# One-core encoder block: activations of 16 FFN blocks turned on VectorE and moved by SBUF transfers

## The reference

```python
hn = _modulate(_rms(h, norm_ffn1[l]), sh1, sc1)
h = h + 0.5 * g1[:, None, :] * _swiglu(hn, ffn1_w1[l], ffn1_w3[l], ffn1_w2[l])
...
hn = _modulate(_rms(h, norm_ffn2[l]), sh3, sc3)
h = h + 0.5 * g3[:, None, :] * _swiglu(hn, ffn2_w1[l], ffn2_w3[l], ffn2_w2[l])
```

## Time and profile before

| | |
|---|---|
| time, median of 3 runs | 2528.01 us (2526.07 to 2530.0) |
| span of the profiled execution | 2528.3 us |
| TensorE busy | 2499.9 us, 99% of the span |
| VectorE busy | 1830.6 us, 72% |
| ScalarE busy | 1159.0 us, 46% |
| read from HBM | 608.43 MB, 242 GB/s over the span |
| transposes of `act_tok` on TensorE | 176 |
| granted TensorE clock, mean | 0.998 of full speed |

### The profile page before, as it was taken

How to read it: one execution, slowest core, us unless ns; L and a number is a source line. 1 busy time by engine, 2 the same in 40 slices (tenths; PEclk the granted TensorE clock), 3 DMA queues, 4 the chain that set the end, 5 groups by cost and what they waited for, 6 DMA issues and landing times.

```text
span 2528.3 us, 33298 instructions
## 1 busy us (share of the span) xinstructions
PE 2499.9 (99%) x12314; PEld 2108.9 (83%) x12314; DVE 1830.6 (72%) x2016; ACT 1159.0 (46%) x1396; POOL 84.0 (3%) x118
## 2 busy tenths in 40 slices
PE   7999999999999999999999999999999999999999
PEld 5778888888888999898888888888888888888887
DVE  6876668898877888887866677776689555555556
ACT  4444444444445555655555444444544444444443
POOL 4210000000000000000100000000000000000000
PEclk9999999999999999999999999999999999999999
DMA  9976579898976777874544778787598655565565
GB/s 370 366 282 194 184 261 344 291 341 291 340 259 210 270 261 268 279 228 152 164 142 138 245 267 272 251 298 243 167 334 301 203 192 190 189 191 188 190 191 173
DMA packets 281219, 614.45 MB, mean 243 GB/s; under 512 B 23586, under 2 KB 24196, under 8 KB 280196
## 3 DMA queue, kind: packets, MB, share of 16 engines
q1 hardware_dynamic: 269600, 571.41, 67.4%
q0 software_dynamic: 9744, 36.73, 3.9%
q10 hardware_dynamic: 1748, 4.62, 0.5%
HBM read 608.43 MB, written 4.25 MB: 242 GB/s over the span
## 4 chain that ended last, share of the span: by engine, by line
PE 95%; DVE 2%; DMA 1%; issue 0%; ACT 0%; ACTq 0%; DVEq 0%
PE psum L2159 27%; PE psum L2161 27%; PE psum L2160 27%; PE psum L2453 3%; PE psum L2455 3%; PE psum L2454 3%; PE psum L2476 2%; PE psum L2147 2%; DMA raw<-in_ffn_w 1%; DVE w_lo L1368 1%; PE psum L2269 0%; DVE ada_acc L1482 0%; DMA badas<-in_b_ada 0%; PE psum L2240 0%; PE psum L2201 0%
## 5 line engine op out<-in xcount | busy, mean ns | idle before, releaser
L1368 DVE TENSOR_TENSOR w_lo<-raw,w_hi 128x1024 fp32r<-128x1024 f32 x850 | 1036.6, 1223 | 518.8 <-ACT w_hi L880 517.6
L880 ACT ACTIVATE w_hi<-raw 128x1024 fp32r<-128x1024 f32 x850 | 899.0, 1060 | 1017.4 <-PE psum L2161 873.5
L2159 PE MATMUL psum<-w_hi,xT_hi 128*128 128x512 f32 x1984 | 784.8, 396 | 6.4 <-issue 4.6
L2161 PE MATMUL psum<-w_hi,xT_lo 128*128 128x512 f32 x1984 | 773.8, 390 | 0.0
L2160 PE MATMUL psum<-w_lo,xT_hi 128*128 128x512 f32 x1984 | 773.5, 390 | 0.0
L2159 PEld LDWEIGHTS psum<-w_hi,xT_hi 128*128 128x128 f32 x1984 | 373.1, 188 | 89.8 <-issue 13.1
L2161 PEld LDWEIGHTS psum<-w_hi,xT_lo 128*128 128x128 f32 x1984 | 372.9, 188 | 78.9
L2160 PEld LDWEIGHTS psum<-w_lo,xT_hi 128*128 128x128 f32 x1984 | 373.2, 188 | 75.8
L2159 PE MATMUL psum<-w_hi,aT_hi 128*128 128x512 f32 x704 | 274.8, 390 | 0.0
L2161 PE MATMUL psum<-w_hi,aT_lo 128*128 128x512 f32 x704 | 274.1, 389 | 0.0
L2160 PE MATMUL psum<-w_lo,aT_hi 128*128 128x512 f32 x704 | 274.0, 389 | 0.0
(11 more groups left out here) (260 smaller groups left out, 1904.6 us busy)
## 6 DMA issues: line engine op xcount, KB each, us to landing
raw<-in_ffn_w SPq DMA_DIRECT2D x528, 512.0 KB, 4.5
ada_raw<-in_w_ada SPq DMA_DIRECT2D x224, 512.0 KB, 5.7
raw<-in_w_in SPq DMA_DIRECT2D x224, 512.0 KB, 3.8
ada_raw<-in_w_ada POOLq DMA_DIRECT2D x32, 512.0 KB, 7.4
ada_more<-in_w_ada POOLq DMA_DIRECT2D x32, 512.0 KB, 7.3
raw<-in_w_br_ssd SPq DMA_DIRECT2D x32, 512.0 KB, 5.3
raw<-in_w_br_att SPq DMA_DIRECT2D x32, 512.0 KB, 4.5
raw<-in_w_out SPq DMA_DIRECT2D x32, 512.0 KB, 5.1
```

Source lines behind the costliest of these rows:

```text
L880: nc.scalar.activation(w_hi[:, n.slot(SPLIT), 0:size], raw[:, n.slot(RAW), 0:size], ACT.Copy).then_inc(hi_ready, 1)
L1368: nc.vector.tensor_tensor(w_lo[:, n.slot(SPLIT), 0:size], raw[:, n.slot(RAW), 0:size], w_hi[:, n.slot(SPLIT), 0:size], ALU.subtract).then_ ...
L2159: nc.tensor.matmul(o, hi[:, kt + k, toks], whi, start=a, stop=False)
L2161: ins = nc.tensor.matmul(o, lo[:, kt + k, toks], whi, start=False, stop=b)
```

## The change

In 16 of the 22 blocks (4 to 9 of the first FFN, 0 to 9 of the second) the eight transposes leave TensorE. In their place:

1. VectorE, right behind the product at u = 2, turns `act_tok` in 32x32 pieces (`turn_bands`): two block transposes of 128x512, one for each half of the tokens, into `act_blk`. Each piece is then turned within itself, but lies on the partitions of its token group.
2. SP, behind the load of unit 6 (`MOVE_AFTER`) and the adaLN load that may follow, waits for `act_blocked` and issues 16 transfers of 32 partitions by 256 values (32 KB) from `act_blk` to `aT_raw`, one for each pair of partition groups (`move_act`).
3. ScalarE at u = 7 waits for all 16 (`act_moved`) and writes `aT_hi` from `aT_raw` in two instructions, one for each half (`moved_hi`); VectorE writes `aT_lo` in two (`moved_lo`).
4. On TensorE the wait for `y_added` that stood before the turn stands before the first w2 unit.

Blocks 0 to 3 of the first FFN and block 10 of both keep the turn on TensorE. `turns(o)` counts the turns that are left.

```diff
+BLOCKED_FROM = (4, 0)
+BLOCKED = tuple(FBLK - 1 - o for o in BLOCKED_FROM)
+BANDS = P // 32
+BAND_DMAS = BANDS * BANDS
...
+    act_blk = place("act_blk", at_temp + 64 * KB, [BANDS, UNIT // BANDS])
+    aT_raw = place("aT_raw", at_temp + 68 * KB, [BANDS, UNIT // BANDS])
...
+    MOVE_AFTER = 6
...
+    def blocked(o):
+
+        f, i = divmod(o.n0, FBLK)
+        return BLOCKED_FROM[f] <= i < FBLK - 1
...
+    def by_tokens(t, half):
+
+        return t[:, :, half * P:(half + 1) * P].rearrange("p k (b t) -> p k b t", t=32)
+
+    def by_bands(half):
+
+        return aT_raw[:].rearrange("p b (k s t) -> p s k b t", s=HALF, t=32)[:, half]
...
+        def move_act(o):
+
+            sp.wait_ge(act_blocked, moves_before(o).count(plus=1))
+            for band in range(BANDS):
+                for to in range(BANDS):
+                    sp.dma_start(aT_raw[32 * to:32 * (to + 1), band, :],
+                                 act_blk[32 * band:32 * (band + 1), to, :]).then_inc(act_moved, 16)
...
                 for u, source in enumerate(pair_of_blocks):
...
+                    o = At(f * FBLK + LOOP_FROM[f] + u // BLOCK, 2, trip)
+                    if blocked(o) and u % BLOCK == MOVE_AFTER:
+                        move_act(o)
...
+        def moved_hi(o, n):
+
+            act.wait_ge(act_moved, moves_before(o).count(plus=1) * 16 * BAND_DMAS)
+            act.wait_ge(unit_done, n.count())
+            for half in range(HALF):
+                ins = nc.scalar.activation(by_tokens(aT_hi, half), by_bands(half), ACT.Copy)
+            ins.then_inc(ahi_ready, 1)
...
                     if u == 7:
-                        act_hi(o)
+                        moved_hi(o, n) if blocked(o) else act_hi(o)
...
+        def turn_bands(o):
+
+            dve.wait_ge(prod_ready, o.count(plus=1))
+            for half in range(HALF):
+                ins = nc.vector.transpose(act_blk[:].rearrange("p c (k s t) -> p s k c t", s=HALF, t=32)[:, half],
+                                          act_tok[:, half, :].rearrange("p (k c t) -> p k c t", c=BANDS, t=32))
+            ins.then_inc(act_blocked, 1)
+
+        def moved_lo(o):
+
+            dve.wait_ge(ahi_ready, o.count(plus=1))
+            for half in range(HALF):
+                ins = nc.vector.tensor_tensor(by_tokens(aT_lo, half), by_bands(half), by_tokens(aT_hi, half), ALU.subtract)
+            ins.then_inc(alo_ready, 1)
...
                     if u == 2 and not after_second:
                         prod(o, n)
+                    if u == 2 and blocked(o):
+                        turn_bands(o)
                     if u == 7:
-                        act_lo(o)
+                        moved_lo(o) if blocked(o) else act_lo(o)
...
                 for u in range(UPB):
-                    if u == 5:
+                    if u == 5 and not blocked(o):
 
                         if adds.n0:
                             pe.wait_ge(y_added, adds.count())
...
                     if q == 0:
                         pe.wait_ge(alo_ready, o.count(plus=1))
+                        if blocked(o) and adds.n0:
+                            pe.wait_ge(y_added, adds.count())
```

More of the change, by code:

```diff
@@ L301, in build @@
     act_turned = sem("act_turned")
+    act_blocked = sem("act_blocked")
+    act_moved = sem("act_moved")
     ahi_ready = sem("ahi_ready")
@@ L515, in rows_cols, with moves_before, turns @@
         return w[row:row + 2 * P, cols].rearrange("(k p) n -> p k n", p=P)
+    def blocked(o):
+        f, i = divmod(o.n0, FBLK)
+        return BLOCKED_FROM[f] <= i < FBLK - 1
+    def moves_before(o):
+        f = o.n0 // FBLK
+        return o + (-BLOCKED_FROM[0] if f == 0 else BLOCKED[0] - FBLK - BLOCKED_FROM[1])
+    def turns(o):
+        before = sum(1 for i in range(o.n0) if not blocked(At(i)))
+        return At(before) if blocked(o) else o + (before - o.n0)
     def span(start, size):
@@ L683, in _ @@
                     load_ada(At(e * KT + k), ada_source(e, k))
+                for i, at in enumerate((FIRST, FIRST + SECOND)):
+                    if f and u == at + MOVE_AFTER:
+                        move_act(At(f * FBLK + i))
             with sp.Fori(0, TRIPS[f]) as trip:
@@ L698, in _ @@
                     load_ada(At(e * KT + k % KT), ada_source(e, k % KT))
+                o = At(f * FBLK + FBLK - 3 + u // BLOCK)
+                if blocked(o) and u % BLOCK == MOVE_AFTER:
+                    move_act(o)
             if f == 1:
@@ L1026, in second @@
                     if u == 7:
-                        act_hi(o, 0)
+                        moved_hi(o, n)
             def hidden(n, o):
@@ L1053, in ffn @@
                 if u == 7:
-                    act_hi(At(o))
+                    moved_hi(At(o), At(n)) if blocked(At(o)) else act_hi(At(o))
                 if u == UPB - 1 + LAG:
@@ L1585, in prod @@
             dve.wait_ge(silu_ready, o.count(plus=1))
-            if o.n0:
-                dve.wait_ge(act_turned, o.count())
+            if o.n0 and not blocked(o + -1):
+                dve.wait_ge(act_turned, turns(o).count())
             nc.vector.tensor_tensor(act_tok[:], silu_a[:], psum[:, bank:bank + HALF, :], ALU.mult).then_inc(prod_ready, 1)
+        def turn_bands(o):
[9 more added lines that the diff above has]
+            ins.then_inc(alo_ready, 1)
         def act_lo(o, bank=4, hi=aT_hi, lo=aT_lo):
@@ L1720, in ffn @@
                     prod(At(o), At(n))
+                    if blocked(At(o)):
+                        turn_bands(At(o))
                 if u == 7:
-                    act_lo(At(o))
+                    moved_lo(At(o)) if blocked(At(o)) else act_lo(At(o))
             n += 2 * UPB
@@ L2413, in ffn @@
             for u in range(UPB):
-                if u == 5:
+                if u == 5 and not blocked(At(o)):
                     pe.wait_ge(y_added, adds)
@@ L2425, in ffn @@
                     pe.wait_ge(alo_ready, o + 1)
+                    if blocked(At(o)):
+                        pe.wait_ge(y_added, adds)
                 if i == 1:
```

7 lines of the change are left out of this document (3 added, 4 removed).

## The result

The changed kernel takes 2562.89 us (median of 4 runs, 2561.27 to 2566.81) against 2528.69 for the kernel before: ratio 1.0139, 95% interval 1.0125 to 1.0153. It is slower by 34 us. The forecast was 2517.

A forecast was written before the change was run, and what follows sets the result against it. The prediction took TensorE to bound the kernel (95% of the chain): 2528.3 - 13.9 for removed transposes + 3.2 for stalls in adaLN blocks = 2517.6 us span, say 2517; range 2511 to 2534.

The forecast's parts named there:

- What is removed: On TensorE, 16 blocks lose their eight transposes, 0.87 us a block by the chain: 13.9 us gained.
- What is added on VectorE and ScalarE: Block transposes 1.5 us and low part in halves 0.1 per block on VectorE; some 0.1 on ScalarE, hidden in gaps.
- rival of dear transposes: On VectorE, scattered 32x32 pieces cost say 5 us a block instead of 1.5: 2548 us; chance 0.06.
- What is added on SP: Sixteen 32 KB transfers per block on SP's queue at 0.45 us an issue: 7.2 us per block.
- the broadcast row: The largest issue measured on SP, 1.07 us, used as upper bound per issue; the range took it only to 0.65.
- The hold: Time SP's queue is taken by the 16 issues in a block, delaying loads behind them: 7.2 us.
- A block with adaLN loads: Eight blocks, six in the first FFN, two in the second: 0.4 us lost in each, 3.2 us in all.
- the cover: Time to spare before late loads stop TensorE: 0.7 and 0.1 us with adaLN loads, 2.4 without.
- A block without adaLN loads: Eight blocks of the second FFN: 2.4 us to spare at unit n+7, so the delay is hidden and nothing lost.
- The sum: Whole kernel: 2528.3 - 13.9 + 3.2 = 2517.6 us for the profiled span, say 2517 for the median.
- SP's hold decides: Rival on SP's queue: 2530 us at 0.60 us an issue, 2569 at 0.75; chance 0.19 for 0.6 or more.
- The DMA engines decide: Rival: backlog drains slower than 1.4 us a load, 1.6 us lost in eight blocks, 2527 us; chance 0.10.

The follow-up runs named there:

- no_moves: The changed kernel without the 16 transfers per block, high and low parts made from act_blk; 2515.21 us, ratio 0.9941.
- hbm_source: The changed kernel with all 16 transfers per block fetched from w_ada in HBM, readers taking act_blk; 2533.28 us, ratio 1.0014.
- spread_4x4: The changed kernel with the 16 transfers issued four behind each of the loads of units n+6 to n+9; 2551.21 us, ratio 1.0086.
- pool_moves: The changed kernel with the same 16 transfers issued by GpSimd instead of SP; 2526.37 us, ratio 0.999.
- twelve_moves: The changed kernel with only the first 12 of the 16 transfers per block, readers taking act_blk; 2533.09 us, ratio 1.0016.
- eight_moves: The changed kernel with only the first 8 of the 16 transfers per block, readers taking act_blk; 2521.71 us, ratio 0.9965.
- bounce: The changed kernel with moves through HBM: four stores behind the load of n+6, one fetch behind that of n+8; 2521.88 us, ratio 0.9973.

## Why the prediction was wrong

**What is removed: right.** 13.9 us forecast; no_moves stands 14.7 below the profiled execution before (2528.3 - 2513.6). The chain's 0.87 us for eight transposes was the right reading; eight times 272 ns would have been 2.5 times too much.

**What is added on VectorE and ScalarE: right where nothing is late.** Two block transposes of 0.69 us, hidden in no_moves. The rival of dear transposes fell. But that VectorE has gaps was read for the first FFN alone, and in the first two blocks of the second it has hardly any: before, it was busy 71.0 of the 75 us from 1870 to 1945, in no_moves 73.3.

**What is added on SP: the price of an issue failed.** I took 0.45 us between the rows of back-to-back issue, and measured is 0.633. The rows were good for what they showed, transfers with an end in HBM (0.46 in a row of 16). The one thing that set the moves apart, both ends in SBUF, I did not count among the unknowns: I compared by shape and size, and the bound from the broadcast row, 1.07, I cut down to 0.65 for the range. The hold became 10.3 us instead of 7.2.

**A block with adaLN loads: the cover failed too.** With the hold as forecast, hbm_source loses 18.4 us (2532.0 - 2513.6), not 3.2. In the first FFN the blocks lose 0.5 to 1.7 us instead of 0.4. The backlog drains more slowly at first than the 1.4 us a load that I took from the best slice of the earlier trace rows (4.1 us from n+7 to n+8), and I followed it only to n+9: in three of the six blocks n+8 and n+9 are in time, and TensorE first stands at n+12 for `y_add`, a wait that the prediction put at nothing after its move. In the first two blocks of the second FFN they lose 4.6 and 5.8, more than half of the whole: I had worked out one block of the first FFN and counted these two like it. Yet the trace of before showed that they had less cover; from 1860 to 1960 us ScalarE waited there for weight loads 8 times, 13.4 us in sum, without any move, and in the blocks of the first FFN never:

```profile
ACT w_hi L880 <- PE psum L2161: 41.4, 26, 1.9
ACT w_hi L880 <- DMA raw<-in_ffn_w: 13.4, 8, 3.0
```

(Waits of ScalarE, kernel before: us in total, times, longest.) These waits cost TensorE nothing: it has no stand in the stretch before, nor in no_moves, where ScalarE has 15 such waits, 23.5 us in sum. Two things set the blocks apart. The holds follow each other after 16 units instead of 24, all with adaLN loads between them; and VectorE is busy 98%, so that it can't catch up on splits that came late. By the trace of hbm_source both play a part, two of the four long stands behind late loads and two behind VectorE's own work; no run varies one without the other, so how much each costs stays open.

**A block without adaLN loads: right.** 2.4 us to spare at a hold of 7.2 means a stall of 0.7 at 10.3; measured 0.85 (66.1 against 65.3), and none at 7.6. The stall was outside the sum only because the hold was taken too short.

**The sum.** Of the 51.5 us that the moves cost, 26 fall on the six blocks of the first FFN, 15 on the first two of the second, 8 on the other eight, and 2 lie outside the blocks (sums of the differences from product to product between the two traces). At 0.633 us an issue my own cover would have given 2.4 to 3.0 us in eight blocks and 0.7 in the other eight, 27 us in all, and a time of 2541 (2528.3 - 13.9 + 27). The overrated cover makes up the other 24 us of the loss. Either error alone takes the gain away: the measured price with my cover gives 2541, and my price with the cover as it is gives 2533, which is hbm_source.

**The rivals.** "SP's hold decides" was the right one in place and mechanism, and it had 0.19. Its size was not right: it gave 2530 at 0.60 us an issue and 2569 at 0.75, which brackets the result, but by the same cover as the forecast it gives 2541 at the measured price. The Trainium skill's rule on small transfers ("DMA: Bandwidth & Descriptors", Rules for kernel authors) pointed the right way, though by the runs it is not the size that costs (a quarter of the bytes changed nothing) but the number of issues. "The DMA engines decide" was not a rival but a second part of the same thing, the backlog that the hold leaves: its 1.6 us a block at the forecast price is near what hbm_source loses in the first FFN (0.5 to 1.7) and far below the 4.6 and 5.8 of the other two.

## What to carry to other kernels

A transfer's price on the queue that issues it is a cost of its own: count the issues, time them by a row with the same ends (SBUF to SBUF is not HBM to SBUF), and then read what stands behind them in that queue. Work out the cover for each stretch with other traffic, not for one block that stands for all; a stretch in which a consumer already waits for its loads has little, and where another engine on the way is busy 98% nothing late is caught up. Follow the lateness past the first consumer too: here it came back four units later, at an addition that stood in VectorE's list behind a late split. And when moves are spread among loads, see who reads them: a reader that waits in order holds everything queued behind it.

## What the hardware showed that I had not expected

- An issue on SP costs 0.63 us when source and destination both lie in SBUF and 0.46 from HBM, in rows of 16: within SBUF for 2, 32 and 64 KB alike, from HBM for 32 and 64, and in both for 32 and 128 partitions. Five transfers by way of HBM were cheaper in all than 16 within SBUF, though they move the data twice and come back later: the fetch takes a median of 7.0 us to land and a move 1.9.
- GpSimd issues the same transfer in 0.50 us, but it lands after 4.1 us (median) instead of 1.9. Part of this may be traffic, since the weight loads run on beside it: issued from SP among the loads, in spread_4x4, it took 3.1.
- A stall of TensorE can cost a second time. After the two stands in the block shown above (0.83 and 1.85 us idle) the granted clock fell to its lower level, 1.2 GHz, and matmuls that otherwise start every 0.23 us started every 0.43, for 3.4 us. This happened in 4 of the 16 blocks of the changed kernel (near 390, 533, 1930 and 1957 us), some 1.7 us of TensorE's time each; in spread_4x4 in 6, in pool_moves in 2, in twelve_moves in 1, in hbm_source, eight_moves and bounce in none. In the first FFN the two blocks with such a fall lose 5.2 and 4.9 us against no_moves and three full ones without it 4.0 to 4.5, so that most of the fall seems to lie beside waiting that would have come anyway.
